# Softplus ahead of a conversion, layer norm on VectorE, two conversions behind the sums at layer ends, and the first units among the x blocks, in a kernel of two transformer blocks

## The chip, the cores and the metric

The kernel runs on one core of a Trainium2 chip, in one launch. Its engines work side by side, each with its own queue of instructions: TensorE (PE, matrix products, results in eight PSUM banks), VectorE (DVE), ScalarE (ACT), GpSimd (POOL) and SyncE (SP, which issues most DMAs). They wait for each other through semaphores. The metric is the device time of one execution in microseconds, lower is better.

## What is computed

256 tokens of width 1024 go through two blocks in float32. Cut to what matters here:

```
x = x + 0.5 * swiglu(rmsnorm(x, ff1_norm), ff1_w_gate, ff1_w_up, ff1_w_down)
h = rmsnorm(x, mix_norm);  proj = h @ w_in
v = layernorm(v, ln_g, ln_b)            # groups of 256 columns, then a mix over positions
z = q @ k.T / 8                         # stick-breaking attention, 16 heads of 64
log_keep = where(causal, -softplus(z), 0)
w = exp(log_sigmoid(z) + reverse_cumsum(log_keep) - log_keep)
x = x + merged @ w_out
x = x + 0.5 * swiglu(rmsnorm(x, ff2_norm), ...)
# second block: attention "moba", MLP, attention "fox", MLP, and a final norm
```

## The kernel before

**Weights.** Every weight matrix is read once, as 448 "units" of up to 128x1024 numbers. SP sends unit c into raw, a ring of RAW = 6 slots; its helper room waits until VectorE has finished with the unit six before. ScalarE's helper hi(c) (L618) copies the unit to w_hi in the rounded type fp32r, and VectorE's lo(c) (L961) subtracts to get the rest, w_lo. Both rings have 8 slots. TensorE then multiplies three times (high by high, high by low, low by high) in three() at L1431, or in the feed-forward's first half at L1517 and L1524, and signals `used`. So ScalarE and VectorE work some four units ahead of TensorE (AHEAD = 4), and each engine goes through its list strictly in the order in which the code is written: what stands behind a waiting instruction waits too.

**The start.** GpSimd builds the matrix ident (L456, L457). TensorE runs ten transposes of ident (L1831), transposes the gains of the first norm (L1833, they come from gain_rows, which ScalarE's queue loads at L605, ahead of the second half of x at L607), runs five more (L1836), and then transposes x in 16 blocks (turn, L1454), 4 in a bank. turned on ScalarE (L656) writes the rounded xt_hi of two blocks of 128 features at a time, turned on VectorE (L996) the rest xt_lo. After four of the eight feature blocks both convert unit 0, after the other four units 1 to 3. When the first feed-forward has run its first units, token_rows (L1487) on TensorE needs diag, which VectorE makes (diagonal, L1057) out of the root mean squares that ScalarE takes (stat, L630).

**Layer ends.** The feed-forwards ff1, ff2 and the MLP mlp0 end in ffn_end. TensorE computes the last product in four units: units 0 and 1 give the left half of the sum, 2 and 3 the right one. Between 2 and 3 it transposes the left half of the new x (turn_x, L1454), for which VectorE must have added the left half to x (add_half, two instructions at L1073). Ahead of add_half VectorE has the last chunk's loop of lo, which converts the first four units of the next layer.

**First attention ("stick").** One cycle for each pair of heads. TensorE: middle(pr) (L1661 to L1665) takes the masked softplus from work[1], then the scores of the next pair, then the weighted sum, then the projections of a later pair (48 products, L1431). ScalarE: Abs, Exp and Ln of the next pair's scores (first_part, L717 to L726), the weights' Exp, then hi(c + 2). VectorE: lo(c + 2), the scaling of q (q_evac, L1089), the softplus of the next pair (second_part, two instructions at L1115), y_lo (L1129), k_evac (L1094), lo(c + 3). GpSimd masks the softplus with affine_select (L468), and TensorE's middle of the next pair waits for that.

**Layer norm.** After the projections a_in VectorE takes mean and variance (L1307, L1310), ScalarE the root (L884), VectorE the reciprocal (L1312) and (v - mean) * rstd in eight groups of 256 columns (L1317). GpSimd multiplies by the gain rows and adds the offset rows, 1024 columns at a time (L567, L569). VectorE goes on with lo of the gate projections' units. The result is used much later, by the mix of positions on TensorE.

## Time and profile before

| | us |
|---|---|
| median of 3 runs | 1244.16 |
| lowest and highest run | 1243.75, 1244.47 |
| profiled execution | 1244.19 |
| its span | 1242.4 |
| TensorE busy in it | 1224.5 (99% of the span) |
| VectorE busy in it | 816.7 |
| ScalarE busy in it | 625.8 |
| GpSimd busy in it | 171.1 |

The span is the time from the first to the last instruction of the profiled execution; 1.8 us lie around it. A row of the timeline gives start and duration in us, engine, line and operation, outputs and inputs, and in brackets how long the engine had stood idle and whom it waited for. Matmuls overlap, so a row's duration is longer than the distance between two starts: with 512 columns they start 0.227 us apart when nothing holds them, with 256 columns 0.12 us.

### The profile page before, as it was taken

How to read it: one execution, taken by the hardware profiler on the slowest of the kernel's cores; microseconds unless marked ns; L12 is line 12 of the kernel's file. 1: busy time of each engine (PE TensorE's matmuls, PEld its weight loads, DVE VectorE, ACT ScalarE, POOL GpSimd, SP SyncE). 2: the span in 40 equal slices, each digit the busy share in tenths (PEclk: the TensorE clock that was granted, in tenths of full speed). 3: DMA queues.
4: the chain of work that ended last, by engine and by line, in shares of the span. 5: the costliest groups of instructions: out<-in, count | busy, mean ns of one | idle time of the engine just before them, and what ended most of it. 6: DMA issues, size and time to landing. Idle time of an engine off the chain costs nothing.

```text
span 1242.4 us, 17592 instructions
## 1 busy us (share of the span) xinstructions
PE 1224.5 (99%) x6847; PEld 1047.5 (84%) x6847; DVE 816.7 (66%) x1229; ACT 625.8 (50%) x965; POOL 171.1 (14%) x224
## 2 busy tenths in 40 slices
PE   8999999999999999999999999999999999999997
PEld 7888888888878888888878988888888888888886
DVE  6766666344676667766676766875765576876764
ACT  6544436554644347444446566544446365744443
POOL 1222210122030003222102310000000541000000
PEclk9999999999999999999999999999999999999999
DMA  7755566533847455655665435865562555675540
GB/s 248 246 180 184 189 201 186 185 105 94 295 132 224 146 170 174 201 192 188 195 195 153 137 119 186 268 189 189 186 200 76 171 164 163 195 252 189 191 147 35
DMA packets 174907, 221.74 MB, mean 178 GB/s; under 512 B 9084, under 2 KB 103896, under 8 KB 174824
## 3 DMA queue, kind: packets, MB, share of 16 engines
q1 hardware_dynamic: 173496, 216.86, 55.2%
q0 software_dynamic: 880, 2.70, 0.8%
q8 instruction: 54, 0.88, 0.3%
q10 hardware_dynamic: 448, 1.05, 0.2%
q14 instruction: 29, 0.24, 0.1%
HBM read 219.52 MB, written 1.06 MB: 178 GB/s over the span
## 4 chain that ended last, share of the span: by engine, by line
PE 88%; DVE 6%; ACT 4%; issue 1%; DMA 0%; POOL 0%; ACTq 0%; DVEq 0%; POOLq 0%
PE bank L1431 48%; PE bank L1517 22%; PE bank L1524 11%; DVE w_lo L961 3%; PE bank L1454 1%; PE bank L1688 1%; ACT w_hi L618 1%; PE bank L1671 1%; PE bank L1661 1%; DVE xt L996 1%; ACT xt L656 1%; DVE x L1073 1%; DVE a_uv L1317 1%; PE bank L1648 1%; PE bank L1646 1%
## 5 line engine op out<-in xcount | busy, mean ns | idle before, releaser
L961 DVE TENSOR_TENSOR w_lo<-raw,w_hi 128x1024 fp32r<-128x1024 f32 (+1 forms) x448 | 499.2, 1137 | 234.3 <-ACT w_hi L618 234.0
L618 ACT ACTIVATE w_hi<-raw 128x1024 fp32r<-128x1024 f32 (+1 forms) x448 | 420.5, 972 | 278.3 <-PE bank L1524 146.6
L1517 PE MATMUL bank<-xt,w_hi 128*128 128x512 f32 x1216 | 316.6, 392 | 0.4 <-ACT w_hi L618 0.4
L1517 PEld LDWEIGHTS bank<-xt,w_hi 128*128 128x128 f32 x1216 | 215.8, 189 | 35.1 <-ACT w_hi L618 0.6
L1524 PEld LDWEIGHTS bank<-xt,w_lo 128*128 128x128 f32 x1216 | 170.6, 190 | 15.3
L1524 PE MATMUL bank<-xt,w_lo 128*128 128x256 f32 x1216 | 175.1, 282 | 0.0
L1431 PE MATMUL bank<-w_hi,xt 128*128 128x512 f32 x512 | 160.1, 394 | 1.9 <-DVE w_lo L961 1.1
L1431 PE MATMUL bank<-w_hi,yt_lo 128*128 128x512 f32 x336 | 132.2, 394 | 0.0
L1431 PE MATMUL bank<-w_hi,yt_hi 128*128 128x512 f32 x336 | 130.9, 390 | 0.0
L1431 PE MATMUL bank<-w_lo,yt_hi 128*128 128x512 f32 x336 | 130.9, 390 | 0.0
L1431 PE MATMUL bank<-xt,w_hi 128*128 128x256 f32 x640 | 115.9, 283 | 0.0
L1431 PEld LDWEIGHTS bank<-w_hi,xt 128*128 128x128 f32 x512 | 94.4, 188 | 24.9 <-issue 4.2
L555 POOL TENSOR_TENSOR work<-work,rbc 128x512 f32<-128x512 f32 x40 | 70.7, 1790 | 249.4 <-DVE work L1014 249.4
L1431 PE MATMUL bank<-w_lo,xt 128*128 128x512 f32 x256 | 99.8, 390 | 0.0
L1431 PEld LDWEIGHTS bank<-xt,w_hi 128*128 128x128 f32 x640 | 99.5, 191 | 0.2
L1014 DVE TENSOR_REDUCE work<-bank 128x256 f32<-128x512 f32 x152 | 94.3, 681 | 0.0
L1431 PE MATMUL bank<-xt,w_lo 128*128 128x256 f32 x320 | 91.8, 287 | 0.0
L1431 PE MATMUL bank<-w_hi,ht_lo 128*128 128x512 f32 x224 | 87.3, 390 | 0.0
L1431 PE MATMUL bank<-w_hi,ht_hi 128*128 128x512 f32 x224 | 87.2, 389 | 0.0
L1431 PE MATMUL bank<-w_lo,ht_hi 128*128 128x512 f32 x224 | 87.2, 389 | 0.0
L1431 PEld LDWEIGHTS bank<-w_hi,yt_lo 128*128 128x128 f32 x336 | 63.1, 188 | 13.9 <-issue 1.0
L1431 PEld LDWEIGHTS bank<-w_lo,yt_hi 128*128 128x128 f32 x336 | 63.1, 188 | 13.3
(198 smaller groups left out, 1202.1 us busy)
## 6 DMA issues: line engine op xcount, KB each, us to landing
raw<-in_w_up SPq DMA_DIRECT2D x64, 512.0 KB, 4.2
raw<-in_w_down SPq DMA_DIRECT2D x64, 512.0 KB, 4.4
raw<-in_w_in SPq DMA_DIRECT2D x56, 512.0 KB, 4.5
raw<-in_ff_w_gate SPq DMA_DIRECT2D x88, 256.0 KB, 2.9
raw<-in_ff_w_up SPq DMA_DIRECT2D x88, 256.0 KB, 3.2
raw<-in_ff_w_down SPq DMA_DIRECT2D x88, 256.0 KB, 4.4
raw<-in_moba_w_qkv SPq DMA_DIRECT2D x24, 512.0 KB, 4.2
raw<-in_w_o SPq DMA_DIRECT2D x16, 512.0 KB, 3.6
```

Of the source, the lines that this page charges most:

```text
L555: pool.tensor_tensor(work[1][:, part, :].rearrange("p (a b) -> p a b", a=2), work[0][:, part, :].rearrange("p (a b) -> p a b", a=2), by_token,
L618: act.activation(w_hi[:, c % RING, 0:w], raw[:, c % RAW, 0:w], ACT.Copy).then_inc(s["hi_ready"], 1)
L656: act.activation(dst[:, k, :], src, ACT.Copy, scale=scale).then_inc(s["tr_hi"], 1)
L961: dve.tensor_tensor(w_lo[:, c % RING, 0:w], raw[:, c % RAW, 0:w], w_hi[:, c % RING, 0:w].bitcast(F32), ALU.subtract).then_inc(s["lo_ready" ...
L996: dve.scalar_tensor_tensor(low[:, k, :], src, gain[:, 8 * g + k:8 * g + k + 1], high[:, k, :].bitcast(F32), ALU.mult, ALU.subtract)\
L1014: dve.tensor_reduce(work[0][:, q // 2, (q % 2) * S:(q % 2 + 1) * S], up_banks(m)[q][:].rearrange("p (a b) -> p b a", a=2), AX_X, ALU.add)\
L1073: dve.scalar_tensor_tensor(v, bank[first + tok][:], by, v, ALU.mult, ALU.add)\
L1317: dve.tensor_scalar(v, v, bn2[:, n, 0:1], ln_rstd[:, n:n + 1], ALU.subtract, ALU.mult)\
L1431: ins = pe.matmul(dst, p, q, start=first and n == 0, stop=last and n == 2)
L1454: ins = pe.transpose(banks[b][:, o:o + P], src[:, tok, k * P:(k + 1) * P], ident[:])
L1517: ins = pe.matmul(up_banks(m)[q][:], w_h[:, k % 2, q * P:(q + 1) * P], flat(xt[:, k, :, :]), start=k == 0, stop=False, skip_group_check=True)
L1524: ins = pe.matmul(up_banks(m)[q][:, 0:S], w_l[:, k % 2, q * P:(q + 1) * P], xt_hi[:, k, :], start=False, stop=k == KT - 1, skip_group_chec ...
```

## The change

Five edits:

1. The gains of the first norm are loaded by GpSimd's queue, as its first instruction, and no longer by ScalarE's.
2. At the start turned and the conversions alternate: two feature blocks of x, unit 0, two blocks, unit 1, and so on, on ScalarE and on VectorE.
3. At the ends of ff1, ff2 and mlp0 VectorE converts two of the next layer's units ahead of add_half of the left half; the third stands behind that, the fourth behind add_half of the right half. (At the end of mlp1 there is no next unit.)
4. In the first attention's cycle second_part stands ahead of q_evac and lo(c + 2).
5. The layer norm is done by VectorE alone in two passes of eight: (v - mean) * gain, then v * rstd + offset. GpSimd's four instructions and the semaphore ln_done2 go.

```diff
+            pool.dma_start(gain_rows[0:8, :], ff1_norm.rearrange("a (k p) -> (a k) p", p=P)).then_inc(s["gain_in"], 16)
             pool.memset(eps[:], EPS).then_inc(s["zero_done"], 1)
...
-            pool.wait_ge(s["blk1_in"], 32)
-            for tok in range(TOK):
-                v = a_uv[:, tok, 0:D]
-                pool.wait_ge(s["ln_done2"], GROUPS * (tok + 1))
-                pool.tensor_tensor(v, v, ln_rows[0], ALU.mult).then_inc(s["lng_done"], 1)
-                pool.wait_ge(s["lng_done"], tok + 1)
-                pool.tensor_tensor(v, v, ln_rows[1], ALU.add).then_inc(s["v_ln"], 1)
...
-            act.dma_start(gain_rows[0:8, :], ff1_norm.rearrange("a (k p) -> (a k) p", p=P))\
-                .then_inc(s["gain_in"], 16)
             act.dma_start(x[:, 1, :], x_in[0, P:2 * P, :]).then_inc(s["x_in"], 16)
...
-            turned("turn_ff1", 0, [(xt_hi, 0)])
-            hi(0)
-            turned("turn_ff1", 1, [(xt_hi, 0)])
-            for u in range(1, AHEAD):
+            for u in range(AHEAD):
+                turned("turn_ff1", u // 2, [(xt_hi, 0)], (u % 2,))
                 hi(u)
...
-                    for u in range(10 if m < n - 1 else 8, 12):
+                    for u in (10, 11) if m < n - 1 else (8, 9):
                         lo(c + u)
...
                 add_half(phase, scale, 0, b - 3)
+                lo(b + 2)
                 between()
                 add_half(phase, scale, 1, b - 1)
+                lo(b + 3)
...
                     first_part(pr + 1)
-                    if kind == "stick":
-                        lo(c + 2)
-                        q_evac(c, e)
-                    elif pr:
+                    if kind != "stick" and pr:
                         y_part(pr - 1)
                     second_part(pr + 1)
-                    if kind != "stick":
-                        q_evac(c, e)
-                        lo(c + 2)
-                    elif pr:
+                    q_evac(c, e)
+                    lo(c + 2)
+                    if kind == "stick" and pr:
                         y_part(pr - 1)
...
-                v = a_uv[:, tok, g * GD:(g + 1) * GD]
-                dve.tensor_scalar(v, v, bn2[:, n, 0:1], ln_rstd[:, n:n + 1], ALU.subtract, ALU.mult)\
-                    .then_inc(s["ln_done2"], 1)
+                cols = slice(g * GD, (g + 1) * GD)
+                v = a_uv[:, tok, cols]
+                dve.scalar_tensor_tensor(v, v, bn2[:, n, 0:1], ln_rows[0][:, cols], ALU.subtract, ALU.mult)\
+                    .then_inc(s["lng_done"], 1)
...
+                dve.wait_ge(s["lng_done"], n + 1)
+                dve.scalar_tensor_tensor(v, v, ln_rstd[:, n:n + 1], ln_rows[1][:, cols], ALU.mult, ALU.add)\
+                    .then_inc(s["v_ln"], 1)
```

VectorE's list at the end of ff1, before: w_lo is a conversion, x<-bank,x is add_half, xt the rest of the transposed x.

```order
L1042 TENSOR_TENSOR ht_lo<-work,ht_hi 128x512 [waits ht_hi]
L961 TENSOR_TENSOR w_lo<-raw,w_hi 128x1024 [waits hi_ready] x4
L1073 SCALAR_TENSOR_TENSOR x<-bank,x 128x512 [waits used]
L1073 SCALAR_TENSOR_TENSOR x<-bank,x 128x512
L996 SCALAR_TENSOR_TENSOR xt<-bank,gain,xt 128x256 [waits tr_hi]
L996 SCALAR_TENSOR_TENSOR xt<-bank,gain,xt 128x256
```

The same place on VectorE in the changed kernel, as far as the conversion of the fourth unit and of the one that follows it:

```order
L1030 TENSOR_TENSOR ht_lo<-work,ht_hi 128x512 [waits ht_hi]
L949 TENSOR_TENSOR w_lo<-raw,w_hi 128x1024 [waits hi_ready] x2
L1061 SCALAR_TENSOR_TENSOR x<-bank,x 128x512 [waits used]
L1061 SCALAR_TENSOR_TENSOR x<-bank,x 128x512
L949 TENSOR_TENSOR w_lo<-raw,w_hi 128x1024 [waits hi_ready]
L984 SCALAR_TENSOR_TENSOR xt<-bank,gain,xt 128x256 [waits tr_hi]
L984 SCALAR_TENSOR_TENSOR xt<-bank,gain,xt 128x256
L984 SCALAR_TENSOR_TENSOR xt<-bank,gain,xt 128x256 [waits tr_hi]
L984 SCALAR_TENSOR_TENSOR xt<-bank,gain,xt 128x256
L1061 SCALAR_TENSOR_TENSOR x<-bank,x 128x512 [waits used]
L1061 SCALAR_TENSOR_TENSOR x<-bank,x 128x512
L949 TENSOR_TENSOR w_lo<-raw,w_hi 128x1024 [waits hi_ready] x2
```

Two of the four conversions ahead of the sum have moved behind it, one behind each half.

VectorE's list in one cycle of the first attention, before: work is the softplus, qt and kt the scaled q and k, yt_lo the rest of the output.

```order
L961 TENSOR_TENSOR w_lo<-raw,w_hi 128x1024 [waits hi_ready] x2
L1089 SCALAR_TENSOR_TENSOR qt<-bank,rbc 128x256 [waits used]
L1115 SCALAR_TENSOR_TENSOR work<-bank,work 128x384 [waits ln_done] x2
L1129 TENSOR_TENSOR yt_lo<-bank,yt_hi 128x256 [waits y_hi]
L1094 TENSOR_TENSOR kt<-bank,rbc 128x256 [waits used]
```

The same cycle on VectorE in the changed kernel (in its first one, without yt_lo):

```order
L1105 SCALAR_TENSOR_TENSOR work<-bank,work 128x384 [waits ln_done] x2
L1079 SCALAR_TENSOR_TENSOR qt<-bank,rbc 128x256 [waits used]
L949 TENSOR_TENSOR w_lo<-raw,w_hi 128x1024 [waits hi_ready]
L1084 TENSOR_TENSOR kt<-bank,rbc 128x256 [waits used]
L949 TENSOR_TENSOR w_lo<-raw,w_hi 128x1024 [waits hi_ready]
```

The softplus now comes first and no longer waits for the conversion, which itself waits for ScalarE's hi.

VectorE's list at the layer norm, before: bn is mean and variance, a_uv holds v.

```order
L1310 BN_AGGR bn<-bn 128x2 [waits bn_done] x8
L1312 RECIPROCAL ln_rstd<-ln_rstd 128x8 [waits lns_done]
L1317 TENSOR_SCALAR a_uv<-a_uv,bn,ln_rstd 128x256 [waits lnr_done]
L1317 TENSOR_SCALAR a_uv<-a_uv,bn,ln_rstd 128x256 x7
L961 TENSOR_TENSOR w_lo<-raw,w_hi 128x1024 [waits hi_ready,gate_in]
```

The same place on VectorE in the changed kernel (work holds the gain and offset rows):

```order
L1294 BN_AGGR bn<-bn 128x2 [waits bn_done] x8
L1296 RECIPROCAL ln_rstd<-ln_rstd 128x8 [waits lns_done]
L1303 SCALAR_TENSOR_TENSOR a_uv<-a_uv,bn,work 128x256 [waits blk1_in,lnr_done]
L1303 SCALAR_TENSOR_TENSOR a_uv<-a_uv,bn,work 128x256 x7
L1310 SCALAR_TENSOR_TENSOR a_uv<-a_uv,ln_rstd,work 128x256 [waits lng_done] x8
L949 TENSOR_TENSOR w_lo<-raw,w_hi 128x1024 [waits hi_ready,gate_in]
```

Sixteen instructions with two tensor inputs stand where eight with one stood, ahead of the same conversion.

## Rows read from the trace of the kernel before

**Rows 1.** Waits of TensorE: waiting line, waited for, us in total, times, longest.

```profile
PE bank L1454 <- DVE x L1073: 3.8, 5, 1.4
PE bank L1661 <- POOL work L468: 2.0, 6, 1.0
...
PE bank L1431 <- DVE w_lo L961: 1.1, 3, 0.5
```

**Rows 2.** Timeline, first attention, TensorE (start, duration, what): first cycle, a later one.

```profile
232.66 0.40 PE L1431 MATMUL bank<-xt,w_hi 128*128 128x256 f32 x2
232.90 0.38 PE L1661 MATMUL bank<-work,ntri 128*128 128x256 f32 x1
...
251.83 0.40 PE L1431 MATMUL bank<-xt,w_hi 128*128 128x256 f32 x2
252.44 0.48 PE L1661 MATMUL bank<-work,ntri 128*128 128x256 f32 x1 [0.21 <-POOL work L468]
```

**Rows 3.** Timeline at the end of ff1, VectorE and TensorE.

```profile
188.49 4.63 DVE L961 TENSOR_TENSOR w_lo<-raw,w_hi 128x1024 fp32r<-128x1024 f32 x4 [0.26 <-ACT w_hi L618]
...
193.04 1.28 DVE L1073 SCALAR_TENSOR_TENSOR x<-bank,x 128x512 f32<-128x512 f32 x2
...
194.38 0.33 PE L1454 MATMUL bank<-ident,x 128*128 128x128 f32 x1 [1.37 <-DVE x L1073]
```

**Rows 4.** Timeline at the end of mlp0: left half's last product, and the sum.

```profile
934.07 0.39 PE L1431 MATMUL bank<-w_lo,yt_hi 128*128 128x512 f32 x1
...
934.57 0.75 DVE L1073 SCALAR_TENSOR_TENSOR x<-bank,rstd_sq,x 128x512 f32<-128x512 f32 x1 [3.14 <-PE bank L1431]
```

**Rows 5.** VectorE on 256 columns (timeline at 196) and on 1024 (line L972).

```profile
196.00 1.66 DVE L996 SCALAR_TENSOR_TENSOR xt<-bank,gain,xt 128x256 fp32r<-128x256 f32 x4 [1.68 <-ACT xt L656]
...
L972 DVE SCALAR_TENSOR_TENSOR x<-x,rstd_f,row_gain x2: 1278/1281/1284, 658.4 to 659.6; 128x1024 f32<-128x1024 f32 x2
```

**Rows 6.** Timeline of the later cycle of rows 2, ScalarE (Ln) and VectorE (softplus).

```profile
247.11 0.94 ACT L726 ACTIVATE work<-work 128x384 f32<-128x384 f32 x2
...
251.27 1.01 DVE L1115 SCALAR_TENSOR_TENSOR work<-bank,work 128x384 f32<-128x384 f32 x2
```

**Rows 7.** Timeline at the layer norm, VectorE and TensorE.

```profile
346.28 6.92 DVE L1317 TENSOR_SCALAR a_uv<-a_uv,bn,ln_rstd 128x256 f32<-128x256 f32 x8
...
353.57 0.39 PE L1431 MATMUL bank<-w_lo,xt 128*128 128x512 f32 x1
...
354.26 3.41 DVE L961 TENSOR_TENSOR w_lo<-raw,w_hi 128x1024 fp32r<-128x1024 f32 x1
...
354.48 0.70 PE L1431 MATMUL bank<-w_hi,xt 128*128 128x512 f32 x2 [0.52 <-DVE w_lo L961]
```

**Rows 8.** Timeline of the start: TensorE and ScalarE's queue, to unit 0.

```profile
0.80 0.59 ACTq L605 DMA_DIRECT2D gain_rows<-in_ff_norm  x1
...
1.69 2.37 PE L1831 MATMUL bank<-ident 128*128 128x128 f32 x10 [1.69 <-POOL ident L457]
...
6.74 3.48 PE L1454 MATMUL bank<-ident,x 128*128 128x128 f32 x16 [1.22 <-DMA x<-in_x]
...
10.58 2.11 PE L1517 MATMUL bank<-xt,w_hi 128*128 128x512 f32 x8 [0.37 <-ACT w_hi L618]
```

**Rows 9.** Timeline to token_rows: a late load, diag, and TensorE's use of it.

```profile
17.01 1.06 ACT L618 ACTIVATE w_hi<-raw 128x1024 fp32r<-128x1024 f32 x1 [0.41 <-DMA raw<-in_ff_w_up]
...
21.12 0.48 DVE L1057 TENSOR_SCALAR work<-ident,rstd 128x128 f32<-128x128 f32 x2
...
22.37 0.61 PE L1487 MATMUL bank<-work,ones 128*128 128x128 f32 x4
```

**Rows 10.** Eight transposes of x later on; two DMA issues on GpSimd.

```profile
199.88 1.04 PE L1454 MATMUL bank<-ident,x 128*128 128x128 f32 x8
...
L585 POOL DMA_DIRECT2D wf<-in_w_f x1: 1100/1100/1100, 470.5 to 470.5; - x1
...
L586 POOL DMA_DIRECT2D bf<-in_b_f x1: 540/540/540, 471.6 to 471.6; - x1
```

More of the change, by code:

```diff
@@ L645, in inverse_root, with turned @@
                 act.activation(dst[:], rms[:], ACT.Exp, scale=-0.5).then_inc(s["rstd_done"], 1)
-            def turned(phase, half, sets):
+            def turned(phase, half, sets, parts=(0, 1)):
                 banks = turn_banks(phase, half)
-                for b in range(2):
+                for b in parts:
                     act.wait_ge(s["tr_ready"], at(phase, "tr_ready") + 2 * half + b + 1)
@@ L981, in final, with turned @@
                     scaled(tok)
-            def turned(phase, half, sets):
+            def turned(phase, half, sets, parts=(0, 1)):
                 banks = turn_banks(phase, half)
-                for b in range(2):
+                for b in parts:
                     dve.wait_ge(s["tr_hi"], at(phase, "tr_hi") + len(sets) * (4 * half + 2 * b + 2))
@@ L1273, in _ @@
             dve.wait_ge(s["gain_cols"], 1)
-            turned("turn_ff1", 0, [(xt_lo, xt_hi, 0)])
-            lo(0)
-            turned("turn_ff1", 1, [(xt_lo, xt_hi, 0)])
-            for u in range(1, AHEAD):
+            for u in range(AHEAD):
+                turned("turn_ff1", u // 2, [(xt_lo, xt_hi, 0)], (u % 2,))
                 lo(u)
@@ L1875, in _ @@
                 tok, g = divmod(n, GROUPS)
-                pe.wait_ge(s["v_ln"], tok + 1)
+                pe.wait_ge(s["v_ln"], GROUPS * (tok + 1))
                 ins = pe.matmul(bank[4 + 2 * tok + g // 2][:, (g % 2) * GD:(g % 2 + 1) * GD], wst[:, g, :],
```

7 lines of the change are left out of this document (6 added, 1 removed).

## The prediction, made before the changed kernel ran

> **What bounds the kernel now.** Read first the share of busy time: TensorE 99% of the span, VectorE, ScalarE and GpSimd at two thirds or less. So a change on the others pays only where TensorE stands still for them, and the next view is the list of TensorE's own waits [rows 1]. It is short: 3.8 us for the new x at layer ends, 2.0 us for GpSimd's masked softplus, 1.1 us for converted weights; beside these it stands at the start, where x and the first unit are late. A wait in these rows is counted behind the modelled end of a matmul, so the loss is larger. In a cycle of the attention that isn't held, the mask's product starts 0.24 us behind the last pair of products, in a held one 0.61 us, a loss of 0.37 us where the row says 0.21 [rows 2]. I add this 0.16 us to each wait of the kind. The third reading is the timeline at each of these places: who was late, and what stood ahead of it in its queue.
>
> **The layer ends.** TensorE starts its transposes at 194.38 and had waited 1.37 us, 1.53 with the 0.16; unheld it would have started at 192.85. VectorE begins the sum for them at 193.04, straight behind four conversions of 4.63 us [rows 3]. The left half's products were done earlier. At the end of mlp0, where VectorE was free, the sum starts 0.50 us after the start of the half's last product [rows 4]. In ff1 six products at 0.227 us (unit 2) lie behind that one, so it started at 192.85 - 7 x 0.227 = 191.26, and the sum could start at 191.76. Are the two remaining conversions done by then? They start at 188.49 and take half of 4.63 us, to 190.8: yes. So the sum comes 1.28 us sooner, and with it the transposes; 0.25 us of the wait stays. ff2's end repeats this with the same wait (both lie in the 3.8 us, the rest of which is elsewhere): 2 x 1.28 = 2.6 us. At mlp0's end the sum waited for TensorE, not for conversions: no gain.
>
> What the moved conversions cost: the third (about 1.2 us) now stands between the sum and the rest of xt, where VectorE stood idle for 1.68 us waiting for ScalarE [rows 5]; that gap covers it. The fourth stands ahead of the next unit's conversion and of the second half's xt. There two conversions fit with some 0.2 us to spare at ff1 and ff2; at mlp0, whose next layer makes twice as many xt, VectorE is that much later, which I put at 0.1 us lost. Each deferred conversion also holds its slot of raw, and SP, waiting in room, sends the units six further on later: by 2 us for one and some 6 us for the other. They are wanted more than 10 us after that, and SP has nothing else behind them but units in the same order. I cost that at nothing; if the cover is gone it shows as ScalarE waiting for a DMA.
>
> **The attention.** ScalarE's Ln of both heads is done at 248.05, but the softplus starts at 251.27 [rows 6], because a conversion stands ahead that waits for ScalarE's hi, which comes behind two more activations. Moved to the front it starts at the latest then. From the softplus's start to TensorE's product, by way of GpSimd's mask, it took 1.17 us (251.27 to 252.44), so now TensorE could have it at 249.2. It wants it at 252.44 - 0.37 = 252.07. The slack is over 2 us, so the wait goes wholly: 2.0 + 6 x 0.16 = 3.0 us [rows 1], 1.16 for the first cycle and 0.37 for each of five more. What could be late instead are q_evac and lo(c + 2), which now stand behind the softplus; q's products, the first half of those that end at 252.1, are done near 249.3 and the softplus at 249.1, so it holds neither. TensorE wants q only after the mask's products, and the unit after those. Bounds: 1.2 us, if only the long wait goes, and 3.0. I take 3.0, because the unheld row stands 0.24 us behind its products [rows 2].
>
> **The layer norm.** VectorE's eight instructions take 6.92 us from 346.28; TensorE needs the next converted unit at 353.57 + 0.23 = 353.80 and gets it at 354.48, 0.68 us late. Two more such waits follow, as a conversion beside GpSimd takes 3.41 us [rows 7], where four alone take 4.63 [rows 3]. All three lose 1.1 + 3 x 0.16 = 1.5 us [rows 1]. Now sixteen instructions replace the eight and GpSimd is out. None like them is in the trace, with two SBUF tensors and 256 columns. The nearest is the xt rest at 256 columns with a column of scalars, four in 1.66 us, so 0.39 us apart; from the 1024-column one, two 1.2 us apart, a quarter is 0.30; at the most each takes its whole 0.48 us [rows 5]. I take 0.40: 16 x 0.40 = 6.4, a hair more for the last, the end is at 352.76. Before, TensorE started 1.28 us after the end of the norm (353.20 to 354.48), so now at 354.04: 0.24 us late instead of 0.68. The next conversions come 1.14 us apart for products that take 2.7: no more waits. Gain 1.5 - 0.24 = 1.3 us; with 0.30 it is 1.5, with 0.48 the end is at 353.96 and it is 0.1.
>
> A rule that would give another sum. The row has 256-column instructions with two tensors 0.39 us apart, one of them in PSUM [rows 5]. The Trainium skill, page VectorE: DVE Perf Modes, section The perf-mode tier table, gives float32 with two tensors in SBUF 2293 ns for 2048 columns, which makes an estimate of 0.29 us for 256 and 4.6 us for sixteen. By it no wait would stay: 1.5 us for this edit and 1236.6 in all. The same table lets the old kind, with one tensor, run at twice that rate, which speaks for leaving it in place; here the eight took 6.92 us, with GpSimd beside them [rows 7]. I stay with the row.
>
> **The start.** Without the gain's DMA, 0.59 us on ScalarE's queue [rows 8], the second half of x is asked for 0.6 us earlier. GpSimd's DMA takes 0.54 to 1.10 us on its own queue [rows 10] and pushes ident and so TensorE's first transposes (1.69) back by as much. TensorE has sixteen small ones at 0.213 us ahead of x, with a little around them 3.8 us: x can start between 6.1 and 6.6 instead of 6.74. The sixteen take 3.48 us, and unit 0 is converted by then, since both engines now turn to it 0.8 us sooner. So unit 0 starts between 9.7 and 10.1 instead of 10.58 [rows 8], 0.5 to 0.9 us sooner. But token_rows, at 22.37, needs diag, done at 21.60, and that hangs on a load that ScalarE waited for until 17.01 [rows 9], which nobody makes faster. So at most 0.7 us pass on. I take 0.6; bounds 0 (the gains arrive late and TensorE waits) and 0.7.
>
> **The sum**, against the profiled execution's 1244.19 us (the median is 1244.16): 2.6 + 3.0 + 1.3 + 0.6 - 0.1 = 7.4 us. 1244.2 - 7.4 = **1236.8 us**.
>
> **The rivals.**
>
> *The clock comes later.* TensorE's transposes of x start 0.213 us apart (3.48 for sixteen, at 1.2 GHz), later ones 0.107 (1.04 for eight with the last one's tail, at 2.4 GHz) [rows 8, 10]; the change comes at 9.9 us. A first stretch of work from 1.69 to 5.5 passed without it. If in the changed kernel, which begins that stretch later, it comes one such stretch of 3.8 us later, the work in it takes twice as long: 1.9 us lost in place of the 0.6. 1236.8 + 0.6 + 1.9 = 1239.3. Against it: the new stretch runs into that of x with no pause of 1.2 us, which should bring the clock sooner rather than later; but then token_rows caps the gain. Chance 10%. By the Trainium skill, page TensorE: Matmul & The Clock Gate, part 1, the number of slow matmuls differs from run to run; no row here shows two runs.
>
> *The short waits stay.* If the 0.37 us of the five later cycles isn't the softplus but something else that switches there, only 1.16 of the 3.0 us come: 1238.6. Against it is the unheld row [rows 2]. Chance 7%.
>
> *The norm gets long* (the other side). One mechanism: sixteen instructions of VectorE in one queue ahead of the conversion that TensorE needs. With d us for each, TensorE starts late by 346.28 + 16d + 1.28 - 353.80, or 16d - 6.2. The change of the whole is that, minus 1.5, minus the 6.1 us gained elsewhere: 16d - 13.8. It is zero at d = 0.86, and slower by 2.5 us at 1.02. If a quarter of the width took as long as the whole, 1.28 us [rows 5], it would be 6.7 us slower, 1250.9. For it: the eight old ones took 0.87 on average [rows 7], but with GpSimd beside them. Against it: 0.39 at 256 columns. Chance 4%.
>
> *The change doesn't do what it says*: other producers are late by as much at the same places (ScalarE's hi or the DMAs behind held slots), and the waits only change their names. Then within 2.5 us of 1244.2. Chance 5%.
>
> **How the numbers follow.** The forecast has 74%: 1236.8, and by its bounds 1236.4 (norm 1.5, start 0.7, no loss at mlp0) to 1238.6 (start 0, norm 0.1); the low end lies 0.9 us under the former, for waits of TensorE too short for the list. The range takes in the late clock: **1235.5 to 1239.6**, and leaves out the last two rivals and some of the tails. A measurement of this kernel tells about 0.2%, 2.5 us, from no change. Faster by more: 91%; within: 5%; slower: 4%.
>
> **What would show it.** In the profile after: the transposes at the end of ff1 wait 0.1 us or less by the row (0.25 us of loss) instead of 1.37; the softplus starts within 0.1 us of Ln, and TensorE's wait for GpSimd's mask is gone from the list; the norm ends near 352.8 less the shift gained before it, and the conversions behind it take 1.2 us each; unit 0 starts near 10.0, and TensorE waits for diag by some tenths if my cap holds. The sum is wrong if TensorE's list shows a new waiting line of over 1 us, if the xt rest at a layer end waits for VectorE, or if ScalarE's hi waits longer for DMAs near 210 us. It is also wrong if a gap closes and the time doesn't follow, which would mean that TensorE isn't the chain there.

## The result, and the profile after

| | before | after |
|---|---|---|
| median, us (runs) | 1244.85 (6) | 1237.58 (6) |
| lowest and highest | 1243.75, 1245.70 | 1236.49, 1238.13 |
| profiled execution, us | 1244.19 | 1236.49 |
| its span | 1242.4 | 1234.8 |

The ratio is 0.994, with a 95% interval of 0.9928 to 0.9953: faster by 5.9 to 9 us. The prediction was 1236.8 us, 0.8 under the median and within its range. That it comes out so close is in part luck: one term has the wrong sign and two others were too small by about as much, so the places have to be read one by one.

TensorE's waits in the changed kernel, counted as in [rows 1]:

```profile
PE bank L1824 <- POOL ident L458: 2.9, 1, 2.9
PE bank L1826 <- DMA gain_rows<-in_ff_norm: 1.3, 1, 1.3
PE bank L1447 <- DVE x L1061: 1.0, 3, 0.3
...
PE bank L1424 <- DVE w_lo L949: 0.4, 1, 0.4
```

The wait for GpSimd's mask is gone, and so are those for conversions behind the norm. The wait for the new x has gone from 3.8 to 1.0 us. But three rows are new or longer: TensorE waits 2.9 us for ident (1.69 before, [rows 8]), then 1.3 us for the gains, and 0.4 us for a conversion in the third attention, where the kernel before has none. The prediction had named a new waiting line of over 1 us as a sign that its sum is wrong; the one for the gains is such a line.

To see what each place gives, take the starts of the same TensorE instruction in both traces (6847 in each, in the same order) and subtract. The difference changes only where a wait or the pace of the products has changed. Changes under 0.05 us are left out, and the change at unit 0 is the sum of what happens between the first transpose and there:

| place (start before, after) | change of the lead, us | lead after it |
|---|---|---|
| first transpose of ident (1.69, 2.92) | -1.23 | -1.23 |
| unit 0 (10.58, 11.13) | +0.68 | -0.55 |
| end of ff1 (194.38, 193.57) | +1.36 | 0.81 |
| attention, first cycle (242.62, 240.65) | +1.26 | 2.07 |
| its five later cycles | 5 x 0.47 | 4.44 |
| norm (354.48, 349.54 and two more) | +1.71 | 6.15 |
| end of ff2 (646.86, 639.35) | +1.36 | 7.51 |
| third attention (959.79, 952.16) | +0.12 | 7.63 |
| third attention (984.15, 976.76) | -0.25 | 7.39 |

Nothing changes at the end of mlp0. The span is 7.6 us shorter; the last 0.2 lie behind TensorE's last instruction.

**Layer end.** The timeline at the end of ff1 after the change, to be laid beside [rows 3]: VectorE and TensorE.

```profile
189.04 2.36 DVE L949 TENSOR_TENSOR w_lo<-raw,w_hi 128x1024 fp32r<-128x1024 f32 x2 [0.26 <-ACT w_hi L608]
...
191.80 0.39 PE L1424 MATMUL bank<-w_lo,ht_hi 128*128 128x512 f32 x1
...
192.22 1.29 DVE L1061 SCALAR_TENSOR_TENSOR x<-bank,x 128x512 f32<-128x512 f32 x2 [0.83 <-PE bank L1424]
...
193.43 1.21 DVE L949 TENSOR_TENSOR w_lo<-raw,w_hi 128x1024 fp32r<-128x1024 f32 x1
193.57 1.09 PE L1447 MATMUL bank<-ident,x 128*128 128x128 f32 x8
...
195.19 1.66 DVE L984 SCALAR_TENSOR_TENSOR xt<-bank,gain,xt 128x256 fp32r<-128x256 f32 x4 [0.55 <-ACT xt L646]
```

Two conversions instead of four stand ahead of the sum, and VectorE is now idle for 0.83 us before it, waiting for TensorE's last product of the left half: in this order of TensorE's list the sum can't be earlier. The third conversion fills most of the gap before the xt rest (0.55 us idle, 1.68 before, [rows 5]).

**Attention.** The first cycles after the change: softplus on VectorE, mask on GpSimd, TensorE's product.

```profile
236.48 0.94 ACT L716 ACTIVATE work<-work 128x384 f32<-128x384 f32 x2
...
237.03 1.02 DVE L1105 SCALAR_TENSOR_TENSOR work<-bank,work 128x384 f32<-128x384 f32 x2 [3.19 <-ACT work L716]
...
237.76 1.59 POOL L469 TENSOR_SCALAR_AFFINE_SELECT work<-work 128x256 f32<-128x256 f32 x4 [7.36 <-DVE work L1105]
...
240.65 0.60 PE L1654 MATMUL bank<-work,ntri 128*128 128x256 f32 x2
241.08 0.38 PE L1656 MATMUL bank<-work,nones 128*128 128x128 f32 x2
```

The mask for both heads is done at 239.35, 1.3 us before TensorE asks. The pair of products at 240.65 is a row of 0.60 us and the next starts 0.43 behind it. The held cycle before:

```profile
252.44 0.70 PE L1661 MATMUL bank<-work,ntri 128*128 128x256 f32 x2 [0.21 <-POOL work L468]
252.97 0.38 PE L1663 MATMUL bank<-work,nones 128*128 128x128 f32 x2
```

There the next one starts 0.53 behind. So a held product costs its wait and, in these rows, another 0.10 us behind it.

**Norm.** The same stretch as [rows 7] after the change.

```profile
341.83 3.26 DVE L1303 SCALAR_TENSOR_TENSOR a_uv<-a_uv,bn,work 128x256 f32<-128x256 f32 x8
345.00 3.26 DVE L1310 SCALAR_TENSOR_TENSOR a_uv<-a_uv,ln_rstd,work 128x256 f32<-128x256 f32 x8
348.17 4.63 DVE L949 TENSOR_TENSOR w_lo<-raw,w_hi 128x1024 fp32r<-128x1024 f32 x4
...
349.13 0.39 PE L1424 MATMUL bank<-w_lo,xt 128*128 128x512 f32 x1
349.54 0.70 PE L1424 MATMUL bank<-w_hi,xt 128*128 128x512 f32 x2
```

Sixteen instructions take 6.34 us, 0.396 us apart, and the conversions behind them run at 1.14 us apart with nobody beside them. TensorE is 0.18 us late once (349.13 to 349.54, where 0.227 is the spacing) and never again.

**Start.** The timeline of the changed kernel, to be laid beside [rows 8].

```profile
0.80 0.40 ACTq L597 DMA_DIRECT2D x<-in_x  x1
...
1.33 0.68 POOL L455 DMA_DIRECT2D gain_rows<-in_ff_norm  x1 [0.83 <-POOLq L1920]
...
2.92 2.37 PE L1824 MATMUL bank<-ident 128*128 128x128 f32 x10 [2.92 <-POOL ident L458]
...
6.55 0.27 PE L1826 MATMUL bank<-ident,gain_rows 8*128 8x8 f32 x1 [1.26 <-DMA gain_rows<-in_ff_norm]
...
7.88 3.50 PE L1447 MATMUL bank<-ident,x 128*128 128x128 f32 x16
```

GpSimd's DMA doesn't begin at 0.80 as those of the other queues do, but at 1.33, and takes 0.68 us; so ident and TensorE's first transpose come 1.23 us later. TensorE gets its 4 KB at 6.55, 5.2 us behind the issue; the second half of x, 512 KB, landed in 5.1 us and before that. By the DMA part of the page:

```profile
x<-in_x ACTq DMA_DIRECT2D x1, 512.0 KB, 5.1
...
gain_rows<-in_ff_norm POOLq DMA_DIRECT2D x1, 4.0 KB, 5.2
```

The DMA packets in the traces say what stood ahead of these 4 KB. In the kernel before the gains were asked for first on ScalarE's queue: their packets start at 1.76 to 2.46, and the last signal of their landing is at 2.82, 2.0 us behind the issue. In the changed kernel both halves of x are asked for ahead of them: x's packets run from 1.82 to 5.52, and those of the gains start only at 5.60. x itself is complete at 5.91 instead of 6.69, so the part of the idea that x comes earlier is true, but its transposes stand behind that of the gains.

### The profile page after: what moved, and what is told of

It is laid out like the page before. It is cut to its first block, busy times and chain, and to the rows that moved or that the text cites. A ratio compares the mean times of both kernels' runs of the same rounds, so it can differ in the third digit from the quotient of the medians.

```text
span 1234.8 us, 17596 instructions
## 1 busy us (share of the span) xinstructions
PE 1222.0 (99%) x6847; PEld 1047.8 (85%) x6847; DVE 812.3 (66%) x1237; ACT 625.6 (51%) x965; POOL 154.3 (12%) x221
## 3 DMA queue, kind: packets, MB, share of 16 engines
HBM read 219.52 MB, written 1.06 MB: 179 GB/s over the span
## 4 chain that ended last, share of the span: by engine, by line
PE 95%; DVE 3%; ACT 1%; DMA 0%; issue 0%; ACTq 0%; DVEq 0%; POOLq 0%
PE bank L1424 55%; PE bank L1510 22%; PE bank L1517 11%; PE bank L1447 1%; PE bank L1681 1%; DVE w_lo L949 1%; PE bank L1664 1%; DVE xt L984 1%; PE bank L1654 1%; PE bank L1641 1%; PE bank L1639 1%; DVE x L1061 0%; PE bank L1685 0%; ACT xt L646 0%; DMA gain_rows<-in_ff_norm 0%; PE bank L1632 0%
```

## The experiments

In all of them the kernel before ran on the same chip: 1244.41 (24 runs) beside e1 to e4, 1244.62 (27) beside e5 to e8, 1244.63 (9) beside e9 to e12. The changed kernel's six runs stand beside 1244.85. So a difference between two medians of changed kernels holds up to 0.4 us of the shift between these groups; where it matters, the traces decide. "Lead" is the difference of starts, as above, against the trace of before.

**Each edit alone.**

e2, the attention's edit alone (edit 4):

```diff
-                    if kind == "stick":
-                        lo(c + 2)
-                        q_evac(c, e)
...
                     second_part(pr + 1)
+                    q_evac(c, e)
+                    lo(c + 2)
```

> The kernel before with the softplus of the first attention ahead of the conversion, and nothing else. Theory: each of the six waits costs its idle time, 0.16 us that the idle time leaves out, and another 0.10 us because the product behind a wait takes 0.33 instead of 0.23 us to the next one; all go: 3.0 + 0.6 = 3.6 us, 1240.6 against 1244.2. Rival (the account in the prediction): 3.0 us, 1241.2. Another: part of it came from the other edits; then less than 2.5 us.

Measured 1241.12 (1240.20 to 1242.63), ratio 0.9975 (0.9964 to 0.9985): 3.3 us faster, which is as far from the theory (3.6) as from its rival (3.0). The trace decides for the theory: the lead grows by 1.26 and five times 0.47, to 3.62 us, and the 0.10 behind each held product is there, six times. 0.4 us of it is lost again in the third attention (below).

e3, the layer ends' edit alone (edit 3):

```diff
-                    for u in range(10 if m < n - 1 else 8, 12):
+                    for u in (10, 11) if m < n - 1 else (8, 9):
...
                 add_half(phase, scale, 0, b - 3)
+                lo(b + 2)
                 between()
                 add_half(phase, scale, 1, b - 1)
+                lo(b + 3)
```

> The kernel before with two of four conversions behind the sums at the ends of ff1, ff2 and mlp0, and nothing else. Theory: 1.35 us at the end of ff1 and as much at that of ff2, nothing or 0.1 us lost at mlp0: 2.7 us in all, 1241.5. Rival: the 0.25 us lost in the last attention of the changed kernel (a conversion waited for at 976.8) comes from the loads that are sent later by this edit; then it shows here at the same place and the gain is 2.4 us.

Measured 1242.06 (1241.00 to 1244.91), ratio 0.9986 (0.9976 to 0.9995): 2.35 us faster. The lead grows by 1.34 and 1.35 at the two ends and by nothing at mlp0's. The median fits the rival's 2.4, and a loss of 0.2 us is there in the third attention. But e2, e4, e5 and e8 lose 0.2 to 1.1 us at the same place and don't have this edit, so it doesn't come from the loads that this edit defers.

e4, the norm's edit alone (edit 5):

```diff
-                dve.tensor_scalar(v, v, bn2[:, n, 0:1], ln_rstd[:, n:n + 1], ALU.subtract, ALU.mult)
+                dve.scalar_tensor_tensor(v, v, bn2[:, n, 0:1], ln_rows[0][:, cols], ALU.subtract, ALU.mult)
...
+                dve.scalar_tensor_tensor(v, v, ln_rstd[:, n:n + 1], ln_rows[1][:, cols], ALU.mult, ALU.add)
```

> The kernel before with the layer norm on VectorE alone, and nothing else. Theory: sixteen instructions 0.40 us apart, 6.4 us, the conversion behind them 0.2 us late instead of 0.7, and the ones after it take 1.2 instead of 3.4 us: 1.7 us gained, 1242.5. Rival: what the trace of the changed kernel shows there depends on the earlier gains; then the waits are still there in part and the gain is under 1 us.

Measured 1243.12 (1241.58 to 1243.92), ratio 0.9987 (0.9978 to 0.9996): 1.3 us faster. At the norm the lead grows by 1.69; in the profiled execution 1.1 us of it is lost again in the third attention (below).

e5, the order of the first units alone (edit 2):

```diff
-            turned("turn_ff1", 0, [(xt_hi, 0)])
-            hi(0)
-            turned("turn_ff1", 1, [(xt_hi, 0)])
-            for u in range(1, AHEAD):
+            for u in range(AHEAD):
+                turned("turn_ff1", u // 2, [(xt_hi, 0)], (u % 2,))
                 hi(u)
```

> The kernel before with the alternation of x blocks and units 0 to 3 at the start, and nothing else; the gains are still loaded by ScalarE's queue ahead of x. Theory: TensorE's transposes of x end at 10.2 as before, unit 0 is converted by then, so it starts at 10.25 instead of 10.58: 0.3 us gained, and token_rows at 22.37 moves by that. Rival: VectorE's later work (copies of the gains, diag) is later by the new order, and token_rows does not move: 0.

Measured 1244.55 (1243.49 to 1245.83), ratio 1.0001 (0.9992 to 1.0010): no difference in the time, though the interval of 1 us either way holds the 0.3 expected as well as the rival's 0. In the trace unit 0 starts at 10.12 instead of 10.58, and the lead behind it is 0.41 us, also at token_rows, so the rival's reason is out. It is still 0.33 at the third attention, where this execution loses 0.74.

e8, the gains on GpSimd's queue alone (edit 1):

```diff
+            pool.dma_start(gain_rows[0:8, :], ...).then_inc(s["gain_in"], 16)
             pool.memset(eps[:], EPS).then_inc(s["zero_done"], 1)
...
-            act.dma_start(gain_rows[0:8, :], ...).then_inc(s["gain_in"], 16)
```

> The kernel before with the load of the first gains on GpSimd's queue, and nothing else. Theory: the gains land at 6.5, x's transposes start at 7.9 instead of 6.7, unit 0 at 11.7 instead of 10.6: 1.1 us lost, 1245.3. Rival: the late gains in the changed kernel's profile were chance; then they land near 4.5 here, x's transposes start near 6.5, and the time is 1244.2 or 0.3 less.

Measured 1245.63 (1245.18 to 1246.44), ratio 1.0008 (0.9999 to 1.0017): 1.0 us slower, with an interval that just takes in no change. In the trace x's transposes start at 8.01 and unit 0 at 11.79, a lead of -1.21. The prediction counted on this edit for a gain; it costs.

**Why the start failed.** e1 is the changed kernel with the gains back on ScalarE's queue:

```diff
-            pool.dma_start(gain_rows[0:8, :], ...).then_inc(s["gain_in"], 16)
...
+            act.dma_start(gain_rows[0:8, :], ...).then_inc(s["gain_in"], 16)
             act.dma_start(x[:, 1, :], x_in[0, P:2 * P, :]).then_inc(s["x_in"], 16)
```

> The changed kernel with one part undone: the gains of the first norm are loaded by ScalarE's queue again, ahead of x. Theory: the start lost time because the gains came late by GpSimd's queue (their transpose starts at 6.55 instead of 3.99, that of x at 7.88 instead of 6.74, unit 0 at 11.13 instead of 10.58). Undone, ident is ready as before (first transposes at 1.7), x is transposed from 6.7, and unit 0 starts near 10.2, since the alternation stays; token_rows starts near 22.0 instead of 22.91. That is 0.7 to 1.0 us faster than the changed kernel, a profiled time near 1235.6. Rival: the start is bound by x and by the clock's rise, not by the gains; then unit 0 stays near 11.1 and the time within 0.3 us of the changed kernel's.

Measured 1236.34 (1235.16 to 1236.58), ratio 0.9932 (0.9919 to 0.9944): 1.2 us below the changed kernel, 0.8 if each is set against the kernel before beside it, where 0.7 to 1.0 were expected. In its trace TensorE begins at 1.69 and never waits for the gains:

```profile
0.80 0.59 ACTq L596 DMA_DIRECT2D gain_rows<-in_ff_norm  x1
...
1.69 2.37 PE L1825 MATMUL bank<-ident 128*128 128x128 f32 x10 [1.69 <-POOL ident L457]
3.99 0.27 PE L1827 MATMUL bank<-ident,gain_rows 8*128 8x8 f32 x1
...
6.63 1.97 PE L1448 MATMUL bank<-ident,x 128*128 128x128 f32 x16 [1.13 <-DMA x<-in_x]
...
9.37 2.08 PE L1511 MATMUL bank<-xt,w_hi 128*128 128x512 f32 x8 [0.77 <-DVE xt L985]
```

Part of this start is chance: e5 has the same one, but its transposes of x are 0.213 us apart and not 0.109, and its unit 0 starts at 10.12 and not at 9.37. Against e5 the changed kernel loses 0.95 us of lead, against e1 1.49.

Two things made the start late: the late ident and the late gains. e10 takes away the first alone, the DMA standing behind the instructions that make ident:

```diff
             const(pool.affine_select(out=ident[:], in_=ident[:], ...))
+            pool.dma_start(gain_rows[0:8, :], ...).then_inc(s["gain_in"], 16)
             const(pool.memset(ones[:], 1.0))
```

> The changed kernel with the gains' DMA still on GpSimd's queue, but behind the two instructions that make ident. Two things made the start late in the changed kernel: TensorE's first transpose came 1.23 us later (ident), and then it waited 1.3 us for the gains. Theory: the gains' landing, 5.2 us behind GpSimd's issue, decides by itself. The first transpose is back at 1.69, the gains land between 6.5 and 7.1 all the same, and x's transposes follow 1.33 us behind them, at 7.9 to 8.4; unit 0 at 11.1 to 11.6; the median 1237.6 to 1238.0, as the changed kernel or a little above. Rival: the late ident is what counts, and x's transposes are back at 6.6, unit 0 at 10.0 and the median at 1236.4, as in e1.

Measured 1238.58 (1237.56 to 1239.33), ratio 0.9951 (0.9936 to 0.9966): slower than the changed kernel by 1.0 us, where at most 0.4 were expected.

```profile
1.84 0.68 POOL L459 DMA_DIRECT2D gain_rows<-in_ff_norm  x1 [0.30 <-POOL ident L457]
...
7.55 0.27 PE L1826 MATMUL bank<-ident,gain_rows 8*128 8x8 f32 x1 [3.50 <-DMA gain_rows<-in_ff_norm]
```

TensorE begins at 1.69 again, and that gains nothing: it waits 3.50 us for the gains, which land 5.7 us behind an issue that begins 0.5 us later. The landing decides, not ident. The rival (1236.4) is out. The sizes of the theory missed too: the gains are there at 7.55 and not by 7.1, x's transposes start at 8.88 and unit 0 at 12.02, and the loss against the changed kernel is 0.87 us at the start. Another 1.1 us of this execution's lag arises in the third attention.

e7 asks what the place is worth when the gains aren't ahead of x at all: they are asked for on ScalarE's queue behind x, and TensorE transposes them behind the first four transposes of x.

```diff
-            pool.dma_start(gain_rows[0:8, :], ...).then_inc(s["gain_in"], 16)
...
             act.dma_start(x[:, 1, :], x_in[0, P:2 * P, :]).then_inc(s["x_in"], 16)
+            act.dma_start(gain_rows[0:8, :], ...).then_inc(s["gain_in"], 16)
...
+                    if b:
+                        middle()
...
-            turn("turn_ff1", x, 0, 1, x_loaded)
+            turn("turn_ff1", x, 0, 1, x_loaded, gain_turn)
```

> The changed kernel with another start: the first gains are loaded by ScalarE's queue behind the second half of x, all fifteen small transposes of ident run first, and the gains are transposed behind the first four blocks of x. Theory: ident is ready at 1.5, x lands at 5.9 as in the changed kernel, and since the gains no longer stand ahead of x, its transposes start near 6.0 and unit 0 near 9.5; token_rows then waits for diag, which hangs on a load, and starts near 21.9. Against the changed kernel's 22.91 that is 1.0 us, and a little more against the kernel before: profiled time near 1235.4. Rival: the clock rises at 9.9 whatever is done, or the gains land late behind x (after 6.8), so that unit 0 is no sooner than 10.2: 0.7 us or less.

Measured 1235.48 (1235.26 to 1236.61), ratio 0.9929 (0.9915 to 0.9942): 2.1 us below the changed kernel. Behind the start its trace is 1.2 us ahead of the changed kernel's and has a lead of 0.7 over the kernel before. This is the 0.6 us of the prediction, got in another way:

```profile
1.25 0.57 ACTq L597 DMA_DIRECT2D gain_rows<-in_ff_norm  x1
...
6.11 1.12 PE L1450 MATMUL bank<-ident,x 128*128 128x128 f32 x4 [0.99 <-DMA x<-in_x]
...
7.16 0.27 PE L1833 MATMUL bank<-ident,gain_rows 8*128 8x8 f32 x1
...
9.83 2.09 PE L1513 MATMUL bank<-xt,w_hi 128*128 128x512 f32 x8
```

x starts at 6.11 (predicted 6.1 to 6.6), unit 0 at 9.83 (predicted 9.7 to 10.1; the theory of e7 itself said 9.5).

e7 also shows that the late landing isn't a matter of GpSimd's queue alone. Here ScalarE's queue brings the same 4 KB, asked for at 1.25 behind both halves of x. Their packets start at 5.20, when most of x has moved (its last packet ends at 5.57), and the last signal of their landing is at 6.33, 5.1 us behind the issue; e9, with the same start, has 6.24. Ahead of x's second half the same queue took 2.0 us. So what the gains stood behind made most of the 5.2 us. No run has them on GpSimd's queue ahead of x, so what the queue adds by itself is known only in part: its issue at 1.33 and the late ident.

**How far the norm may go.** The rival on the other side said: sixteen instructions ahead of a conversion make TensorE late by 16d - 6.2 (d is the time of one in us). e6 adds eight more of the same kind, whose results nothing reads:

```diff
+            for n in range(TOK * GROUPS):
+                ...
+                dve.scalar_tensor_tensor(dst, a_uv[:, tok, cols], bn2[:, n, 0:1], ln_rows[0][:, cols],
+                                         ALU.subtract, ALU.mult)
```

> The changed kernel with eight more instructions of the first pass's kind in the layer norm, written to places that nothing reads; they change nothing that is computed. It measures the slope of the prediction's formula for a long norm. Theory: they take 0.40 us each, TensorE's wait behind the norm grows from 0.2 to 3.4 us, and the time by 3.2 us over the changed kernel, profiled time near 1239.7. Rival: TensorE's lead of several converted units hides part of it; then less than 2 us.

Measured 1241.97 (1240.94 to 1243.32), ratio 0.998 (0.9971 to 0.9989): 4.4 us above the changed kernel where 8 x 0.396 = 3.2 were expected. TensorE behind the wait:

```profile
353.06 1.19 PE L1430 MATMUL bank<-w_hi,xt 128*128 128x512 f32 x2 [3.19 <-DVE w_lo L949]
354.04 0.63 PE L1430 MATMUL bank<-w_lo,xt 128*128 128x512 f32 x1
354.47 1.06 PE L1430 MATMUL bank<-w_hi,xt 128*128 128x512 f32 x2
...
356.63 0.62 PE L1430 MATMUL bank<-w_hi,xt 128*128 128x512 f32 x2
```

The products start 0.43 us apart up to 356.17 and 0.227 from then on. From 353.06 to there it is 3.11 us, and 1.68 in the changed kernel: 1.43 us more on top of 3.18. The table of stretches (columns: stretch, length, busy time and count of PE, PEld, DVE, ACT, POOL, granted clock, DMA share, GB/s) names the cause:

```profile
345.00:349.40 4.40, 4.40 (x21) 3.66 (x20) 4.40 (x13) 1.98 (x2) 0.00 (x0) 1.00 0.00 0
353.00:356.40 3.40, 3.35 (x9) 2.70 (x9) 3.40 (x4) 0.00 (x0) 0.00 (x0) 0.54 0.62 193
356.40:360.00 3.60, 3.60 (x17) 3.00 (x16) 1.95 (x3) 2.96 (x4) 0.00 (x0) 1.00 0.94 332
```

The granted clock is 0.54 behind the wait of 3.19 us, that is near the lower level of 1.2 GHz, and 1.00 ahead of it and later. This wait costs more than itself. e11 adds four instead of eight:

```diff
+            for n in range(4):
+                dve.scalar_tensor_tensor(work[2][:, n // 2, ...], a_uv[:, 0, cols], bn2[:, n, 0:1],
+                                         ln_rows[0][:, cols], ALU.subtract, ALU.mult)
```

> The changed kernel with four more instructions of the same kind in the layer norm (their results go to a scratch buffer that nothing reads; nothing of the computation changes). With eight more TensorE waited 3.2 us by the row, and its next seven products started 0.43 us apart instead of 0.227, which is 1.2 GHz in place of 2.4 and 1.4 us more than the wait. Theory: the clock falls only behind the long wait. With four more, 4 x 0.396 = 1.6 us, TensorE waits 1.8 us, its products stay 0.227 us apart as behind the waits of 1.3 to 1.8 us in the kernel before, and the time is 1.6 to 1.7 us over the changed kernel: 1239.3. Rival: the clock falls here too, and the products behind the wait cost another 1.4 us: 1240.7.

Measured 1239.19 (1238.20 to 1239.58), ratio 0.9954 (0.9942 to 0.9966): 1.6 us above the changed kernel, as the theory said. The first product behind the wait, and the same view of the stretch:

```profile
351.75 0.70 PE L1428 MATMUL bank<-w_hi,xt 128*128 128x512 f32 x2 [1.61 <-DVE w_lo L949]
...
351.70:355.00 3.30, 3.25 (x14) 2.73 (x15) 3.30 (x4) 0.00 (x0) 0.00 (x0) 1.00 0.68 185
```

A wait of 1.61 us leaves the granted clock at 1.00.

**What the single edits don't add up to.** The medians of e2 to e4 give 3.3 + 2.35 + 1.3 = 6.9 us, the places in the traces 3.62 + 2.69 + 1.69 = 8.0. In the third attention something takes some of it back, and it differs from one execution to the next. TensorE waits there for the second of two conversions (the same instructions stand there in every kernel here):

```profile
975.24 2.81 DVE L949 TENSOR_TENSOR w_lo<-raw,w_hi 128x1024 fp32r<-128x1024 f32 x2
975.70 2.59 POOL L516 COPY vn<-side 128x256 f32<-128x256 f32 x2
...
976.76 0.39 PE L1424 MATMUL bank<-xq_hi,w_lo 128*128 128x256 f32 x1 [0.37 <-DVE w_lo L949]
```

These are rows of the changed kernel. In e1 GpSimd comes a little earlier against VectorE:

```profile
973.75 3.96 DVE L950 TENSOR_TENSOR w_lo<-raw,w_hi 128x1024 fp32r<-128x1024 f32 x2
...
973.86 0.74 POOL L515 COPY vn<-side 128x256 f32<-128x256 f32 x2
...
976.20 0.38 PE L1425 MATMUL bank<-xq_hi,w_lo 128*128 128x256 f32 x1 [1.30 <-DVE w_lo L950]
```

Both engines are held: GpSimd's two copies take 1.26 and 1.38 us in the changed kernel, where they take 0.39 and 0.40 with nothing beside them (e9, below); in e1 it is the instruction behind the copies that takes 1.69 us, where it takes 0.61 at other times.

Two conversions take 2.36 us alone. Here they took 2.57 (before, no wait), 2.55 (e6, none), 2.61 (e12, 0.26), 2.76 (e3, 0.33), 2.80 (e8, 0.36), 2.81 (after, 0.37), 2.91 (e7, 0.58), 3.13 (e2, 0.47), 3.53 (e5, 0.88), 3.72 (e11, 1.06), 3.74 (e10, 1.41), 3.86 (e4, 1.21) and 3.96 (e1, 1.30). GpSimd's moment hangs on the DMAs that bring its rows (it waited 4.71 us for them in e7, 6.39 in the changed kernel), VectorE's on TensorE. e9 is e7 with GpSimd's first copy held until both conversions are done:

```diff
+                if phase == "fox" and pr == 0:
+                    pool.wait_ge(s["lo_ready"], RING + at("fox", "units") + 14)
                 pool.tensor_copy(vn[:, e, :, :], side[:, :, ds(pr * P, P)]).then_inc(s["v_done"], 1)
```

> The kernel of e7 with one wait more: in the third attention (fox) GpSimd's first copy to vn waits for VectorE's conversions of units 12 and 13. Theory: in every trace so far TensorE waits 0 to 1.3 us for the second of these two conversions (0.58 in e7, 0.37 in the changed kernel), because GpSimd's copy and bias instructions run beside them and they take 2.57 to 3.96 us where two take 2.36 us undisturbed; how much depends on when the DMAs of the bias rows land. With the copy held the two take 2.4 us, the wait is gone, and the median is 0.5 us below that of e7: 1235.0. Rival: the held copy makes GpSimd's biases late and VectorE waits for them in the next cycle: 1235.5 to 1236.5. Nothing of the computation changes.

Measured 1235.50 (1235.25 to 1235.78), ratio 0.9927 (0.9914 to 0.9939).

```profile
974.17 2.35 DVE L952 TENSOR_TENSOR w_lo<-raw,w_hi 128x1024 fp32r<-128x1024 f32 x2
...
976.69 0.74 POOL L517 COPY vn<-side 128x256 f32<-128x256 f32 x2 [2.13 <-DVE w_lo L952]
```

The conversions take 2.35 us, the wait is gone, and nothing later is late: the lead goes undiminished to the end, 8.70 us. So the collision is the cause of the wait, and the rival's reason, late biases, doesn't show. The profiled execution is 0.3 us faster than that of e7 (1235.50, 1235.79), but the median is that of e7 and not 0.5 us lower; only the spread is smaller, 0.5 us in place of 1.35, of five runs each. What else took the gain back in the median isn't settled.

e12 has edits 3, 4 and 5 together on the kernel before; its diff is the sum of those of e2, e3 and e4.

> The kernel before with edits 3, 4 and 5 and without edits 1 and 2. Theory: the gains read at the places in the trace, 2.7 at the two layer ends, 3.6 in the attention and 1.7 at the norm, add up undiminished: 8.1 us, less some tenths for the wait behind GpSimd's copies in the third attention: 1236.5. Rival: the medians of the three single edits, 2.4, 3.3 and 1.3 below the kernel before, are the true gains: 6.9 us, 1237.5. By the theory this kernel is 1 us faster than the changed one, by the rival the same.

Measured 1237.29 (1235.74 to 1239.32), ratio 0.9941 (0.9928 to 0.9953). The profiled execution was the fastest of the five, 1235.74: there the leads add up whole (1.34 + 3.68 + 1.70 + 1.35, and 0.37 at the start, 8.44 in all at the end of ff2). The median lies near the rival, and five runs spread over 3.6 us. Between the two it decides nothing: added up, the edits give all of it in one execution and 1 us less in the median. For the same reason the median doesn't show that edits 1 and 2 cost anything together (7.3 us below the kernel before, with them and without); the traces show that they do.

## Why the prediction was right where it was, and where it wasn't

**The layer ends: right.** 2 x 1.28 = 2.6 us predicted, 2 x 1.36 measured in the changed kernel, 2.69 in e3. The sum could start at 191.76 by the prediction; with the 0.55 us of the start it starts at 192.22, and it is now TensorE that it waits for. It starts 0.42 us behind the last product and not 0.50, and that is the difference. Of the loss that should stay (0.25 us) 0.18 is left. The deferred loads cost nothing, as said. The 0.1 us that I took off for mlp0 isn't there.

**The attention: mechanism right, term too small.** 3.0 us predicted, 3.63 measured (3.62 in e2). The long wait gave the 1.16 and the later cycles 0.37 each (the last one 0.35). What the term missed is the 0.10 us by which the product behind a held one comes later, six times. I had compared one start with the product ahead of it [rows 2] and not looked at the one behind.

**The norm: right in the part that was a choice, too small in the same way.** I took 0.40 us for an instruction from the row of 0.39 [rows 5]; the trace shows 0.396. The rule of the Trainium skill, page VectorE: DVE Perf Modes, section The perf-mode tier table, from which I had made an estimate of 0.29 us, gives too little for this instruction here; the table's row is for tensor_tensor, and this is another instruction. TensorE's remaining lateness was put at 0.24 and is 0.18. The gain is 1.71 us and not 1.3: of the three waits the later two had their own restart, 0.11 us and more, which I had again left out. And my 1.1 + 3 x 0.16 is 1.6 and not 1.5.

**The start: this step failed, and in its sign.** The prediction has "GpSimd's DMA takes 0.54 to 1.10 us on its own queue and pushes ident [...] back by as much", and a gain of 0.6, "bounds 0 (the gains arrive late and TensorE waits)". Measured is a loss of 0.55, outside the bounds. Two errors. The bounds stopped at 0, though the same sentence names a wait that could take any length: nothing excluded a loss. And the landing had no number: I had rows for the issue [rows 10] and none for the time from issue to landing, and I didn't ask what the load would stand behind. On ScalarE's queue the gains stood ahead of the second half of x and landed in 2.0 us; behind both halves they took 5.2 us on GpSimd's queue and 5.1 on ScalarE's (e7). x did come earlier, as said, by 0.8 us, and nothing could use it. Edit 1 costs 1.2 us (e8), edit 2 gives some 0.4 (e5) to 0.7 of it back. The cap by token_rows, which I put at 0.7 us, isn't a fixed one: in e1 0.95 us of lead pass it, of 1.25 ahead of it, and in e7 0.65 of 0.77.

**The sum** was 7.4 us and is 7.39 at TensorE's last instruction. The error of the start, -1.15, is made up by +0.6 (attention), +0.4 (norm) and the small ones. That these cancel is luck: the extra 0.10 us behind a held product has nothing to do with the landing of a DMA. The 0.8 us between 1236.8 and the median lie elsewhere: the profiled execution of before, on which I built, is 0.2 to 0.7 us faster than the medians measured since (1244.41 to 1244.85) and had no wait at all for that conversion in the third attention, and that of after was the fastest of its six.

**The rivals.** *The clock comes later* has part of a case: x's transposes stay 0.213 us apart to their end (11.08) in the changed kernel and change at 9.8 us in the kernel before. My estimate is that this costs some 0.1 us here, not 1.9: VectorE's xt for unit 0 is done at 10.87, unit 0 started 0.15 us behind that in e1, and here it starts at 11.13. *The short waits stay* is out by the five times 0.47. *The norm gets long* is right as a mechanism (e11: +1.6 for 4 x 0.396; at d = 0.396 it gives 0.14 us late, measured 0.18) and too cheap beyond that (e6: 4.4 for 3.2). *The change doesn't do what it says* is out: the waits are gone from the places named. In the third attention a wait of 0.4 us is new.

## What to carry to other kernels

Price a DMA that is moved by its landing in the new place, not by its issue: ask which loads it then stands behind (4 KB took 2.0 us ahead of x's second half and 5.1 to 5.7 behind both halves) and who waits for it first. A move that freed one queue by 0.6 us cost 1.2 here. When a held matmul is read, compare the start behind it too, and count the waits and not their length alone: five short waits gave back 0.47 us each where the row said 0.2. And where an estimate's lower bound is "nothing gained", say what keeps it from being a loss.

## What the runs showed of the hardware that was not expected

- A 4 KB load behind two of 512 KB came last. From GpSimd's queue it landed 5.2 to 5.7 us behind its issue (changed kernel, e6, e8, e10, e11), from ScalarE's queue 5.0 to 5.1 (e7, e9), beside 512 KB loads that took 5.1. Asked for on ScalarE's queue at 0.80, ahead of the second half of x, it took 1.9 to 2.0 us (e1, before). The Trainium skill, page DMA: Bandwidth & Descriptors, section Anatomy of one DMA, gives some 2 us for the fixed part on GpSimd's path; the measured landing there is more than twice that, and since ScalarE's queue shows the same behind x, the load ahead explains most of it. What makes a load wait for one of another queue isn't shown.
- GpSimd's issue of that DMA begins at 1.33 us, where those of SP and ScalarE begin at 0.80, and takes 0.68 us; ident is made 1.23 us later by it (changed kernel).
- TensorE's clock at the start differs between executions, and it isn't tied to the start of its work. In e1 and e12 x's transposes are 0.109 us apart from the second on (e1: from 6.8 us), in the others they are 0.213 apart up to 9.6 us or later. The granted clock column shows 1.00 at both spacings, so that this is the step between 2.4 and 1.2 GHz is read from the spacing alone. The Trainium skill, page TensorE: Matmul & The Clock Gate, part 1, says that the number of slow matmuls differs from run to run; these traces agree (before and e12 have the same start, and so have e1 and e5). What an edit of the start is worth hangs on it: in e12, without edit 2, transposes that were done at 8.6 us led to a wait of 1.4 for ScalarE's w_hi, and unit 0 started at 10.22; in e1, with it, at 9.37.
- In the middle of the kernel a wait of 3.19 us brought the granted clock to 0.54 for the next 3 us (1.43 us lost), and waits of 1.0 to 1.61 us did not (granted clock 1.00 behind each). One execution shows the fall, and nothing between 1.61 and 3.19 was tried.
- VectorE's conversions from two SBUF tensors and GpSimd's instructions hold each other up: two conversions took 2.35 (e9) to 3.96 us (e1) by how they fell together, and two copies of GpSimd 0.74 (e9) to 2.59 (changed kernel).
